# Context feed-forward: the high and low part of an activation block as one 512-column matmul into the two halves of a PSUM bank, added by VectorE

## What is computed

```
def swiglu(y, w_in, w_out):
    a, b = jnp.split(y @ w_in, 2, axis=-1)
    return (jax.nn.silu(a) * b) @ w_out
...
        xc = ada_out(xc, swiglu(ada_in(xc, modc, 0, norm_pre[l, 0]), ffn_w_in[l, 0], ffn_w_out[l, 0]),
                     modc, 0, norm_post[l, 0], 0.5)
```

## Time and profile before

| | |
|---|---|
| median of 3 runs | 3003.55 us (3003.47 to 3006.01) |
| profiled execution, span from first to last instruction | 3002.8 us |
| profiled execution, own time | not listed apart from the span |
| PE busy | 2963.0 us (99%), 14767 matmuls |
| PE weight loads busy | 2491.8 us (83%), 14767 |
| DVE busy | 1785.7 us (59%) |
| ACT busy | 1128.1 us (38%) |
| POOL busy | 226.3 us (8%) |
| DMA | 383.83 MB, mean 128 GB/s |

### The profile page before, as it was taken

One profiled execution on the slowest core, in us unless ns is written; L12 is line 12 of the kernel. 1 busy time (PEld: TensorE's weight loads), 2 busy tenths in 40 slices (PEclk: granted clock), 3 DMA queues, 4 the chain that ended last, 5 costly groups with the idle time before them and its releaser, 6 DMA issues. The chain is left out here.

```text
span 3002.8 us, 36219 instructions
## 1 busy us (share of the span) xinstructions
PE 2963.0 (99%) x14767; PEld 2491.8 (83%) x14767; DVE 1785.7 (59%) x2589; ACT 1128.1 (38%) x1690; POOL 226.3 (8%) x184
## 2 busy tenths in 40 slices
PE   7999999999999999999999999999999999999999
PEld 6888888888888888888888899888899866788887
DVE  7767666765867667677757656323357656443233
ACT  4433332433424333333434344222235556332222
POOL 0300000000001201100000011000011014100000
PEclk9999999999999999999999999999999999999999
DMA  7454355344433433344443344232235230123221
GB/s 287 152 183 141 126 182 196 126 141 136 144 126 114 152 120 121 109 148 140 148 136 137 133 134 162 98 99 93 97 126 173 91 126 8 57 92 98 98 97 65
DMA packets 107781, 383.83 MB, mean 128 GB/s; under 512 B 11964, under 2 KB 13372, under 8 KB 107616
## 3 DMA queue, kind: packets, MB, share of 16 engines
q1 hardware_dynamic: 83856, 296.51, 29.5%
q10 hardware_dynamic: 23760, 85.01, 8.7%
HBM read 379.37 MB, written 2.10 MB: 127 GB/s over the span
## 5 line engine op out<-in xcount | busy, mean ns | idle before, releaser
L1888 DVE TENSOR_TENSOR WL<-stage,WH 128x1024 fp32r<-128x1024 f32 x508 | 630.5, 1243 | 563.1 <-ACT WH L1256 562.9
L455 PE MATMUL ps<-HH,WH 128*128 128x512 f32 x2184 | 853.4, 391 | 0.3 <-DVE WL L1888 0.3
L456 PE MATMUL ps<-HL,WH 128*128 128x512 f32 x2184 | 850.2, 389 | 0.0
L457 PE MATMUL ps<-HH,WL 128*128 128x512 f32 x2184 | 849.9, 389 | 0.0
L1256 ACT ACTIVATE WH<-stage 128x1024 fp32r<-128x1024 f32 x512 | 537.6, 1053 | 440.7 <-PE ps L457 429.1
L455 PE MATMUL ps<-GH,WH 128*128 128x512 f32 (+2 forms) x1649 | 572.0, 347 | 2.6 <-DVE SCR L2557 1.8
L456 PE MATMUL ps<-GL,WH 128*128 128x512 f32 (+2 forms) x1649 | 569.0, 345 | 0.0
L457 PE MATMUL ps<-GH,WL 128*128 128x512 f32 (+2 forms) x1649 | 569.0, 345 | 0.0
L457 PEld LDWEIGHTS ps<-HH,WL 128*128 128x128 f32 x2184 | 409.9, 188 | 85.8
L455 PEld LDWEIGHTS ps<-HH,WH 128*128 128x128 f32 x2184 | 410.1, 188 | 83.6 <-issue 1.4
L456 PEld LDWEIGHTS ps<-HL,WH 128*128 128x128 f32 x2184 | 410.2, 188 | 82.7
(11 more groups left out here) (265 smaller groups left out, 2905.1 us busy)
## 6 DMA issues: line engine op xcount, KB each, us to landing
stage<-ws SPq DMA_DIRECT2D x535, 512.0 KB, 3.3
MST<-wm ACTq DMA_DIRECT2D x154, 512.0 KB, 3.3
Z<-wm SPq DMA_DIRECT2D x10, 512.0 KB, 7.9
TAB<-consts ACTq DMA_DIRECT2D x7, 448.0 KB, 3.5
MST<-wm SPq DMA_DIRECT2D x6, 512.0 KB, 7.2
out<-X SPq DMA_DIRECT2D x8, 256.0 KB, 2.2
X<-xT SPq DMA_DIRECT2D x4, 256.0 KB, 5.2
X<-xT ACTq DMA_DIRECT2D x4, 256.0 KB, 5.5
```

What stands on the lines that cost most here:

```text
L455: e.matmul(o, wh, mh, start=start, stop=False, **more)
L456: e.matmul(o, wh, ml, start=False, stop=False, **more)
L457: return e.matmul(o, wl, mh, start=False, stop=stop, **more)
L1888: e.tensor_tensor(wl, src, wh.bitcast(F32), ALU.subtract).then_inc(wlo.sem, wlo.up(("w", i)))
```

## The change

GH and GL become the two halves of one tensor G2, so that one access pattern can read a high block and its low block as 2 x 256 columns. In the context's `swiglu`, apart from the pair that `lin2` makes, the matmuls of WH with the high and with the low activations become one of 512 columns, into the two halves of a bank; that of WL with the high ones (256 columns) goes into the first half. Someone then has to add the two halves. DVE does: after "sa" and after "sb" a `tensor_reduce` (function `halves_sum`) adds them into a SCR buffer; silu and the multiply now work in SBUF. In the second projection a `tensor_reduce` writes ZC in half 0, in place of ACT's copy, and in half 1 DVE adds first one half and then the other to ZC.

```
+        def hc_pair(k):
+            a = (k % 2) * 256
+            return G2[:, :, 14 + k // 2, a:a + 256]
+
+        def slot_pair(i):
+            return G2[:, :, i, 0:C]
+
+        def in_halves(who, half, jj):
+            return who == "c" and (half > 0 or jj > 0)
...
+            def mm_halves(o, wh, wl, pair, start, stop):
+                e.matmul(o.rearrange("p (a b) -> p a b", a=2), wh, pair, start=start, stop=False)
+                return e.matmul(o[:, 0:C], wl, pair[:, 0], start=False, stop=stop)
```

On ACT, in step jj:

```
-                    act.wait_ge(mm, "sa", who, half, jj)
-                    e.activation(T, bank("sa", who, half, jj)[:, 0:n], ACT.Silu).then_inc(ev.sem, ev.up(("sa", who, half, jj)))
+                    if in_halves(who, half, jj):
+                        act.wait_ge(dv, "sa2", who, half, jj)
+                    else:
+                        act.wait_ge(mm, "sa", who, half, jj)
+                    e.activation(T, T if in_halves(who, half, jj) else bank("sa", who, half, jj)[:, 0:n], ACT.Silu).then_inc(ev.sem, ev.up(("sa", who, half, jj)))
```

On ACT, for tile nn of the second projection:

```
+                    if half == 0 and who == "c":
+                        continue
```

On DVE, between `step("sa", ...)` and `step("sb", ...)` of jj:

```
+                    if in_halves(who, half, jj):
+                        freed_by, freed = sa.before("sa", who, half, jj) or ("plo", ("shid", who, half, jj - 1))
+                        dve.wait_ge(signals[freed_by], *freed)
+                        dve.wait_ge(mm, "sa", who, half, jj)
+                        halves_sum(bank("sa", who, half, jj), SA("sa", who, half, jj)[:, 0:C], "sa2", who, half, jj)
```

On DVE, after `step("sb", ...)`:

```
+                    if in_halves(who, half, jj):
+                        other = SA("sa", who, half, jj)[:, C:2 * C]
+                        halves_sum(bank("sb", who, half, jj), other, "sb2", who, half, jj)
+                        dve.wait_ge(dv, "sb2", who, half, jj)
+                        dve.wait_ge(ev, "sa", who, half, jj)
+                        made(e.tensor_tensor(T, other, T, ALU.mult), "sb", who, half, jj)
```

On DVE, for tile nn of the context:

```
+                        if half:
+                            dve.wait_ge(dv, "sd", who, 0, nn)
+                            made(e.tensor_tensor(z, p[:, 0:C], z, ALU.add), "sd1", who, nn)
+                            dve.wait_ge(dv, "sd1", who, nn)
+                            made(e.tensor_tensor(z, p[:, C:2 * C], z, ALU.add), "sd", who, 1, nn)
+                        else:
+                            halves_sum(p, z, "sd", who, 0, nn)
```

More of the change, by code:

```diff
@@ L11 @@
 ACT = mybir.ActivationFunctionType
+AX = mybir.AxisListType
 S = 512
@@ L882, in swiglu @@
                 upto["ticks", who, half] = walk.ticks
+                hidden = hc_pair if who == "c" else None
+                wide = S if who == "c" else n
                 for jj in range(11):
                     j0 = half * 11 + jj
-                    p0 = take_bank(("sa", who, half, jj), ev, "sa", who, half, jj)
+                    p0 = take_bank(("sa", who, half, jj), *((dv, "sa2") if in_halves(who, half, jj) else (ev, "sa")), who, half, jj)
                     if jj == 0 and ready:
@@ L891, in swiglu @@
                     else:
-                        lin(("sa", who, half, jj), 8, lambda k: ("ffn_w_in", f, k * 128, j0 * 128), mov, p0[:, 0:n])
-                        p1 = take_bank(("sb", who, half, jj), dv, "sb", who, half, jj)
-                        lin(("sb", who, half, jj), 8, lambda k: ("ffn_w_in", f, k * 128, (22 + j0) * 128), mov, p1[:, 0:n])
+                        lin(("sa", who, half, jj), 8, lambda k: ("ffn_w_in", f, k * 128, j0 * 128), mov, p0[:, 0:wide],
+                            pair=hidden)
+                        p1 = take_bank(("sb", who, half, jj), dv, "sb2" if in_halves(who, half, jj) else "sb", who, half, jj)
+                        lin(("sb", who, half, jj), 8, lambda k: ("ffn_w_in", f, k * 128, (22 + j0) * 128), mov, p1[:, 0:wide],
+                            pair=hidden)
                 if (who, half) == ("c", 1):
@@ L897, in swiglu @@
                 for nn in range(8):
[L898 removed]
+                    p = take_bank(("sd", who, half, nn), dv if half or who == "c" else ev, "sd", who, half, nn)
                     lin(("sd", who, half, nn), 11, lambda k: ("ffn_w_out", f, (half * 11 + k) * 128, nn * 128),
[L900 removed]
+                        lambda k: slot(k, n), p[:, 0:wide], lambda k: ("shid", who, half, k), lows=low_by(who),
+                        pair=slot_pair if who == "c" else None)
             token_mix(0)
@@ L2352, in hidden_low, with halves_sum @@
                     low(GL[:, jj, 0:n], SA("sa", who, half, jj)[:, 0:n], GH[:, jj, 0:n], "shid", who, half, jj)
+                def halves_sum(p, to, *name):
+                    made(e.tensor_reduce(to, p[:, :].rearrange("p (a b) -> p b a", a=2), AX.X, ALU.add), *name)
                 def step(*name):
@@ L2370, in swiglu @@
                     dve.wait_ge(mm, "sb", who, half, jj)
-                    dve.wait_ge(ev, "sa", who, half, jj)
-                    made(e.tensor_tensor(T, bank("sb", who, half, jj)[:, 0:n], T, ALU.mult), "sb", who, half, jj)
+                    if in_halves(who, half, jj):
[4 more added lines that the diff above has]
+                        made(e.tensor_tensor(T, other, T, ALU.mult), "sb", who, half, jj)
+                    else:
+                        dve.wait_ge(ev, "sa", who, half, jj)
+                        made(e.tensor_tensor(T, bank("sb", who, half, jj)[:, 0:n], T, ALU.mult), "sb", who, half, jj)
                 if n == S:
@@ L2379, in swiglu @@
                     step("sd", who, half, nn)
-                    if half:
+                    if who == "c":
+                        z, p = zt(nn), bank("sd", who, half, nn)
+                        dve.wait_ge(mm, "sd", who, half, nn)
+                        if half:
[3 more added lines that the diff above has]
+                            made(e.tensor_tensor(z, p[:, C:2 * C], z, ALU.add), "sd", who, 1, nn)
+                        else:
+                            if nn == 0:
+                                dve.wait_ge(modv, "m", len(MODS) - 1)
+                            halves_sum(p, z, "sd", who, 0, nn)
+                    elif half:
                         z = zt(nn)
```

13 lines of the change are left out of this document (7 added, 6 removed).

## The result

| | before | changed |
|---|---|---|
| median | 3003.55 us (3002.52 to 3006.01, 5 runs) | 3015.9 us (3015.77 to 3022.62, 5 runs) |
| ratio of the times | | 1.0049, 95% interval 1.0038 to 1.006 |
| span of the profiled execution | 3002.8 us | 3014.0 us |
| context half 0, first matmul to `x`'s first | 98.57 us | 103.17 us |
| `x` half 0 and half 1 | 359.07 us | 359.05 us |

The account below looks back on a forecast made before the run. PE was taken as the bound, 99% busy, with DVE near holding it up in half 1. Half 1 +2.1, half 0 -2.4 and coupling +1.0 gave +0.7 us on the median 3003.55: 3004.3 us, range 2999.0 to 3011.0.

Parts of the forecast that it names:

- gain of 512 matmuls: Context blocks on PE, both halves: one matmul less per block saves 13.3 ns, 512 times, 6.8 us.
- volume on DVE, half 0: Context half 0, jj 3 to 8: 8 reductions, 4.9 us, of which 0.9 us is lost (0 to 2.6).
- volume on DVE, half 1: Context half 1: 10 reductions in jj 2 to 8 delay PE's chunk 3.5 us, last part loses 0.3; half 1 +2.1 net.
- coupling: Loaded context stretches: silu waits for DVE's reduction, with WH and a square behind silu; 1.0 us added (0 to 2).
- the reduction's step: DVE in the context: each reduction takes 0.61 us to the next start, like an op reading 512 elements.
- the places of the new waits: PE before WL: 2 to 5 us more idle in half 1 around jj 5 to 8, around one in half 0.
- The rival on this: Context matmuls on PE: two separate halves of the moving operand eat the saving, no gain, 3008.4 us; 4%.
- the chunk of 2267.64: PE chunk in half 1 with 0.19 us spare before the change; forecast to start 3.5 us later.
- ACT and DVE in lockstep: Half 1 jj 2 to 8, half 0 jj 3 to 8: 1.2 us idle per SSQ, about 6 us on top, 3010 us; 16%.
- Its deciding mark: Lockstep rival's sign in the loaded stretches: most SSQs behind a reduction show a wait of 1 us or more.
- Slow reduction: Same two loaded stretches: a reduction takes 1.15 us, adding 9.7 us, 3014 us; 8%.

Follow-up runs that it names:

- PE's part alone: Kernel before with only PE's context blocks as one 512- and one 256-column matmul, DVE and ACT unchanged, some products left out; 3000.36 us against 3003.71.
- volume alone: Changed kernel with all reductions, but silu waits for PE alone and the reduction for silu; 3009.62 us, ratio 1.0023 to the kernel before.
- streams: PE's part alone plus matmul streams without waits behind the last store: 0.120 us per 256 columns, 0.227 per 512, 0.353 a pair by turns.

## Why the prediction was wrong

By its steps, the sizes taken from the stage lengths:

| term | forecast | measured | from |
|---|---|---|---|
| gain of 512 matmuls | -6.8 us | -3.1 | PE's part alone against before |
| volume on DVE, half 0 | +0.9 | +1.84 | volume alone, over PE's part |
| volume on DVE, half 1 | +5.6 | +6.85 | the same (forecast: +2.1 over before, and the 3.5 of gain) |
| coupling | +1.0 | +7.25 | changed kernel over volume alone, both stages |
| sum of both stages | +0.7 | +12.8 | |

- **Right:** PE as the bound; the reduction's step, 0.60 us where 0.61 was assumed; the places of the new waits, half 1 and half 0's middle; `x`'s stages untouched; half 1 as the dearer half.
- **The step that failed most: "In the loaded stretches I add 1.0 us (0 to 2)" for the new coupling.** It is 6.25 of the 12.1 us missed. The text beside it had the mechanism ("Where DVE runs behind, ACT is held with it, and then DVE waits for ACT") but priced it as a small addition. The sum had already spent DVE's idle time on the reductions: 0.8 us of waits for WH and half of the waits for squares. The coupling keeps that idle time in being, so both could not be had: in the window of half 1 DVE is idle 3.82 us, before 3.93. With none of the idle time swallowed the forecast's own figures give, as an estimate, 6.1 - 0.2 + 0.3 - 1.7 = +4.5 us in half 1 and 5.8 - 1.4 - 3.3 = +1.1 in half 0, 3009.2 us. That is nearer, and still 7 us short: 3.7 of them are the gain, below, and the rest no run takes apart.
- **Second: the gain.** 13.3 ns beside the columns is what neighbours of one size show, and the forecast carried it over to a stream of alternating sizes, where a pair costs 6.5 ns more. The rival on this had named the wrong cause (two separate runs of columns, which cost nothing), and its end (no gain at all) was not reached. The Trainium skill (TensorE: Matmul & The Clock Gate, section "Wait — 56ns, not 53.3ns?") has about 2.5 ns per matmul, from which the prediction made an estimate of 1.3 us. That lay 1.8 us below the measured 3.1, the forecast 3.7 above. At equal sizes the streams show 13.3 ns again.
- **Third: the volume, 2.2 us short.** The forecast let half 1's waits end with the chunk of 2267.64, its last part lose 0.3 us and half 0 0.9. The place was right: with the volume alone PE waits 4.88 us in six waits, of which the last, at 2272.60, is at that same chunk. But the last part has 1.69 us, at 2315.87, where before it had 0.81, and half 0 lost 1.84. A WL was priced at 1.23 us; that three of them would take 2.31 was in no term, though the earlier trace rows show one of 2.32 already.
- **The rival "ACT and DVE in lockstep"** had the right mechanism and the right places, a price of about 6 us on top, and gave 3010 us. Its deciding mark, a wait of 1 us or more at most SSQs, did not come: in the loaded part of half 1 the waits are 1.36, 0.63, 0.63 and 1.36 us, and all SSQ waits in the context stages sum to 6.7 us against 6.1 before. The mark was ill chosen. The waits did not have to grow; they had to stop being slack. And in half 0 the idle time that the coupling keeps up is mostly WL's wait for WH, which this rival's price left out: seven waits from 1782 to 1831, of 0.84 to 1.50 us, 9.1 us in all, where the same WLs with the volume alone wait 0.35. What decides is whether the idle time shrinks when work is added. The rival's price is near the measured 7.25, but it came on the same sum, with its gain too large.
- **Slow reduction:** refuted, 684 ns.

Two things stay open. The coupling costs more in half 0 (4.48 us) than in half 1 (2.77), though DVE is less loaded there. The traces name two parts, the waits for WH just told and the slow WLs, of which half 1 has 2.3 us less than the volume alone; but no run separates them. And what PE does between matmuls of unlike size is known only by its 6.5 ns.

## What to carry to other kernels

When an in-order engine gets a wait on a second one that is nearly full, look at what stands behind the waiting instruction, and put what others need ahead of it; here one call moved on ACT took away 7 of 12 us by the medians, 9 by the stages. Don't credit an engine's idle time to new work before asking who ends that idle time: if the new wait ties that engine to the one being loaded, the idle time can stay, as it did here, with the new work on the path beside it. A per-matmul share read from a stream of equal sizes holds for equal neighbours; measure the mixed stream first, and where PE waits for nothing, group matmuls by size.

## What the hardware showed that was not expected

- Matmuls of 512 and 256 columns by turns take 0.353 us a pair, grouped by size 0.347 (streams), in the kernel 0.353 and 0.349. It is the same for a moving operand of one run of 512 columns and of two runs of 256 (stages equal to 0.01 us, and 0.353 us a pair in both streams).
- A WL, 1.22 us elsewhere, took 2.31 us where it started 0.44 us behind POOL's addition to X (the rows of `volume` above). Why these and not others was not tested.
- An operation on DVE that waits for the reduction ahead of it starts 0.71 us after the reduction's start, where an independent one starts after 0.60 (2240.27 to 2240.98, and 2236.55 to 2237.15, in the changed kernel): about 0.1 us for the dependence.

```profile
2236.55 0.68 DVE L2384 TENSOR_REDUCE SCR<-ps 128x256 f32<-128x512 f32 x1
2237.15 0.74 DVE L2332 SCALAR_TENSOR_TENSOR SCR<-Z,RC,ps 128x512 f32<-128x512 f32 x1
...
2240.27 0.68 DVE L2384 TENSOR_REDUCE SCR<-ps 128x256 f32<-128x512 f32 x1
2240.98 0.43 DVE L2413 TENSOR_TENSOR SCR<-SCR 128x256 f32<-128x256 f32 x1
```
